# A two-layer decoder trunk on one core: two modulation products are multiplied earlier, with a seventh slot for weights

## The reference

```python
def ada_params(c, w, b):
    return jax.nn.silu(c) @ w + b

def modulate(x, shift, scale):
    return x * (1.0 + scale[:, None, :]) + shift[:, None, :]

def post_norm_residual(x, y, gate, g, b):
    return layer_norm(DEEPNORM_ALPHA * x + (1.0 + gate[:, None, :]) * y, g, b)

def grouped_moe(...):          # 16 experts, 2 per token, both from the best of 4 groups
    ...
    for e in range(N_EXPERTS):
        a = jax.nn.silu(t @ w_gate[e]) * (t @ w_up[e])
        out = out + gates[:, e:e + 1] * (a @ w_down[e])

for l in range(DEPTH):
    mod = ada_params(c, ada_w[l], ada_b[l])
    sh_a, sc_a, g_a, sh_f, sc_f, g_f = jnp.split(mod, 6, axis=-1)
    if l < N_A:
        h = modulate(x, sh_a, sc_a)            # forgetting attention, 16 heads
        ...
    else:
        if l == N_A:
            kv_sh, kv_sc = jnp.split(ada_params(c, kv_ada_w, kv_ada_b), 2, axis=-1)
            hk = modulate(x, kv_sh, kv_sc)     # keys and values of layer 1
            ...
        h = modulate(x, sh_a, sc_a)            # differential attention, 8 heads
        ...
    x = post_norm_residual(x, y, g_a, ln_attn_g[l], ln_attn_b[l])
    h = modulate(x, sh_f, sc_f)
    m = grouped_moe(h, ...)
    x = post_norm_residual(x, m, g_f, ln_ffn_g[l], ln_ffn_b[l])
```

## Time and profile before

| | us |
|---|---|
| median of 3 runs | 898.19 (897.6 to 899.9) |
| the profiled execution | 900.95 |
| its span, of which all rows speak | 899.3 |
| PE busy | 834.7 (93%) |
| DVE busy | 376.0 (42%) |
| transfers, mean rate | 339 GB/s |

### The profile page before, as it was taken

One profiled execution on the slowest core, in us unless ns is written; L12 is line 12 of the kernel. 1 busy time (PEld: TensorE's weight loads), 2 busy tenths in 40 slices (PEclk: granted clock), 3 DMA queues, 4 the chain that ended last, 5 costly groups with the idle time before them and its releaser, 6 DMA issues.

```text
span 899.3 us, 10792 instructions
## 1 busy us (share of the span) xinstructions
PE 834.7 (93%) x3730; PEld 393.0 (44%) x3730; DVE 376.0 (42%) x927; ACT 127.1 (14%) x341; POOL 90.3 (10%) x146
## 2 busy tenths in 40 slices
PE   6899999999998998899979999999999999889984
PEld 3584675435333333333328557654533333333331
DVE  2185867475211221222148688828521122212215
ACT  1001243011100000000010114611110000010010
POOL 1000000051110001011004000215111110000000
PEclk9999999999999999999999999999999999999998
DMA  8999982019999999999999799405499999999901
GB/s 352 431 421 426 399 329 95 1 59 431 426 428 426 425 427 426 427 426 426 425 384 419 299 426 425 175 0 213 163 406 424 428 424 427 426 427 426 392 12 47
DMA packets 23408, 304.59 MB, mean 339 GB/s; under 512 B 2720, under 2 KB 3232, under 8 KB 5280
## 3 DMA queue, kind: packets, MB, share of 16 engines
q1 hardware_dynamic: 22752, 303.14, 80.6%
q10 hardware_dynamic: 576, 0.40, 0.1%
HBM read 302.49 MB, written 1.05 MB: 338 GB/s over the span
## 4 chain that ended last, share of the span: by engine, by line
PE 68%; DMA 21%; DVE 8%; issue 2%; POOL 1%; ACT 1%; POOLq 0%; DVEq 0%; ACTq 0%
PE ps L1724 17%; DMA ring<-in_moe_w_up_dram 12%; PE ps L1732 7%; PE ps L1558 6%; PE ps L1529 6%; PE ps L1542 6%; PE ps L1642 5%; PE ps L1737 4%; DMA stream<-in_moe_w_up_dram 3%; DMA ring<-in_ada_w_dram 3%; DMA ring<-in_moe_w_down_dram 3%; PE ps L1453 1%; PE ps L1431 1%; PE ps L1705 1%; PE ps L1465 1%
## 5 line engine op out<-in xcount | busy, mean ns | idle before, releaser
L1724 PE MATMUL ps<-ring,hT 128*64 128x512 f32 x384 | 172.4, 599 | 11.8 <-DMA ring<-in_moe_w_up_dram 9.9
L1725 PE MATMUL ps<-ring,hT 128*64 128x512 f32 x384 | 172.7, 600 | 0.0
L1233 DVE TENSOR_TENSOR arena<-arena,ps 128x256 f32<-128x256 f32 x32 | 13.5, 421 | 233.8 <-ACT arena L802 126.8
L1724 PEld LDWEIGHTS ps<-ring,hT 128*64 128x64 f32 x384 | 51.1, 138 | 117.4 <-issue 117.4
L1732 PE MATMUL ps<-ring,arena 128*64 128x512 f32 x208 | 94.8, 599 | 0.0
L1733 PE MATMUL ps<-ring,arena 128*64 128x512 f32 x208 | 94.8, 598 | 0.0
L414 DVE SCALAR_TENSOR_TENSOR spare<-ring,csig,spare 128x512 f32<-128x512 f32 x112 | 86.1, 769 | 3.8
L1737 PE MATMUL ps<-arena 128*128 128x512 f32 x144 | 66.6, 605 | 3.2 <-DVE arena L1242 3.2
L1724 PE MATMUL ps<-spare,hT 128*64 128x512 f32 x128 | 58.9, 609 | 2.7 <-DMA stream<-in_moe_w_up_dram 2.5
L1725 PE MATMUL ps<-stream,hT 128*64 128x512 f32 x128 | 58.9, 610 | 0.0
L1529 PE MATMUL ps<-hT,ring 128*128 128x256 f32 x256 | 57.2, 386 | 1.5 <-ACT hT L680 1.5
(11 more groups left out here) (281 smaller groups left out, 1083.3 us busy)
## 6 DMA issues: line engine op xcount, KB each, us to landing
ring<-in_moe_w_down_dram SPq DMA_DIRECT2D x26, 2048.0 KB, 21.8
ring<-in_ada_w_dram SPq DMA_DIRECT2D x24, 2048.0 KB, 14.7
ring<-in_moe_w_gate_dram SPq DMA_DIRECT2D x24, 2048.0 KB, 18.4
ring<-in_moe_w_up_dram SPq DMA_DIRECT2D x24, 2048.0 KB, 21.3
spare<-in_moe_w_gate_dram SPq DMA_DIRECT2D x8, 2048.0 KB, 23.2
stream<-in_moe_w_up_dram SPq DMA_DIRECT2D x8, 2048.0 KB, 25.3
ring<-in_fox_w_in_dram SPq DMA_DIRECT2D x6, 2048.0 KB, 9.8
ring<-in_kv_ada_w_dram SPq DMA_DIRECT2D x4, 2048.0 KB, 13.8
```

Source lines behind the costliest of these rows:

```text
L1724: t.matmul(ps[0:CAP, bank, :], lhs(k), wcols(ng)[:, k, :], start=(k == 0), stop=(k == KC - 1))
L1725: mm = t.matmul(ps[CAP:P, bank, :], lhs(k), wcols(nu)[:, k, :], start=(k == 0), stop=(k == KC - 1))
```

## The change

- Group 4's pieces stand before the first layer's experts in the list, so they are loaded and multiplied (in `turn_stream(0)` and `route(0)`) where group 3 was; group 3 is multiplied among the last heads of the first attention, in two halves.
- The second piece of the output weights, `N_WO[0][1]`, no longer takes a ring slot but a seventh slot (`HALVES`) of four quarters: both rows of `lnw`, the second half of h, and `fold`. It comes in four transfers.
- The rows of norm 0, whose room that is, are loaded in `expert_loads` ahead of piece e3, once that piece is used.
- `gained` takes block 0 first and waits for each block's rows alone; it stands ahead of `number_slots`. `residual` waits in that order.
- ACT modulates all eight chunks of block 0, DVE only the last four of block 1.
- In `turn_stream(1)` four matmuls on constants (`idle_work`) stand in the product's place; `turn_mod(4)` and its `mod_cols` are gone from there.
- The last two pieces of the experts in layer 0 take ring slots, as they did in layer 1, and the rows of norm 1 and the gate bias come ahead of the key weights.
- An overflow round turns `oput` before it folds gate and up, and gates its output with one DVE instruction from a copy, `gate_halves`.

```diff
@@ the list
     ada(3, 0, 1, 2, 3)
     cols(N_WO[0], fox_w_o, 0, 0, 1)
+    ada(4, 0, 1, 2, 3)
     experts_pieces()
-    ada(4, 0, 1, 2, 3)
...
-            if n == first + 3 * NE - (0, SPARES)[l]:
+            if n == first + 3 * NE - SPARES:
                 free = [s for s in free if s < RING]
-        s = free.pop(0)
+        s = HALVES if n == N_WO[0][1] else free.pop(0)
...
+        def quarter_pieces():
+            return [lnw[:, 0, :], lnw[:, 1, :], h[:, 1, :], fold[:, :, :].rearrange("p a n -> p (a n)")]
@@ SP
+            def load_quarters(n):
+                for s_ in range(2):
+                    sp.wait_ge(ht_ready[s_], HT_N[0][s_])
+                sp.wait_ge(f_steps, 1)
+                for q, part_ in enumerate(quarter_pieces()):
+                    sp.dma_start(part_, pieces[n][:, 1024 * q:1024 * q + 1024]).then_inc(full[HALVES], 16)
...
+                        if l == 0 and 6 * i + j == 3:
+                            spent(sp, N_WO[0][1])
+                            norm_rows(0)
...
-                if n == N_WO[0][0]:
-                    norm_rows(0)
...
             gate_bias(2)
+            sp.wait_ge(x_ready, NB)
+            norm_rows(1)
             for n in range(N_MOE[0] + 3 * NE, N_MOE[1]):
-                if n == N_ADA[5][0]:
-                    sp.wait_ge(x_ready, NB)
-                    norm_rows(1)
@@ POOL
-                pool.wait_ge(xn_r, 4 * (norm + 1))
-                for b in (1, 0):
+                for b in range(NB):
+                    pool.wait_ge(xn_r, 4 * norm + 2 * b + 2)
...
             inv_std(0)
+            gained(0)
             number_slots(0)
-            gained(0)
@@ ACT
-                    act.wait_ge(ht_mm, 4 * norm + 2 * b + 1)
-                    for k in range(4):
+                    for k in range(KC if b == 0 else 4):
+                        if k % 4 == 0:
+                            act.wait_ge(ht_mm, 4 * norm + 2 * b + k // 4 + 1)
@@ DVE
                     gate_weights(0, 1, 0)
+                    mod_rows(3)
                     gate_weights(0, 1, 1)
             nothing_added()
             mod_cols(2, 4)
+            mod_cols(3, 7)
             gate_row(1, 5)
-            fold_cols(1)
+            for m in (1, 2):
+                fold_cols(m)
...
-                            for q, rows in enumerate((slice(0, 64), slice(64, P))):
-                                d.tensor_tensor(oy[rows, :], ps[rows, 7, :], gbc[rows, 1, 512 * q:512 * q + 512],
-                                                ALU.mult).then_inc(o_dve, 1)
+                            d.tensor_tensor(oy, ps[:, 7, :], gate_halves, ALU.mult).then_inc(o_dve, 1)
@@ PE
                 if norm == 1:
-                    mod_product(4, range(0, 5))
+                    idle_work(4, 7)
                 for b in range(NB):
                     if b and norm == 0:
-                        mod_product(3, range(0, 2))
-                    if b and norm == 1:
-                        mod_product(4, range(5, KC))
+                        mod_product(4, range(0, 2))
...
-                pe.wait_ge(x_ready, 2 * NB * l + 2 - b)
+                pe.wait_ge(x_ready, 2 * NB * l + b + 1)
...
+                if p == PAIRS_H - 1:
+                    mod_product(3, range(0, 4))
...
             fox_values(PAIRS_H - 3)
+            mod_product(3, range(4, KC))
...
             turn_mod(2, 4)
+            turn_mod(3, 7)
...
             stream_turned(2)
-            turn_mod(4, 0)
```

More of the change, by code:

```diff
@@ L105, in build @@
     SPARES = 2
+    HALVES = RING + SPARES
     SLOT, TURN = [], []
-    turns, free = [0] * (RING + SPARES), list(range(RING))
+    turns, free = [0] * (RING + SPARES + 1), list(range(RING))
     for n in range(len(pieces)):
-        for l, first in enumerate(N_MOE):
+        for first in N_MOE:
             if n == first + RING:
                 free = [RING + i for i in range(SPARES)] + free
-            if n == first + 3 * NE - (0, SPARES)[l]:
+            if n == first + 3 * NE - SPARES:
                 free = [s for s in free if s < RING]
-        s = free.pop(0)
+        s = HALVES if n == N_WO[0][1] else free.pop(0)
         SLOT.append(s)
@@ L238, in build @@
         oy = part(P, 512)
+        gate_halves = part(P, 512)
         oputT = fold[:, 1, 0:S]
@@ L251, in build @@
         ogu = mrow[:, 1, :]
-        full = [sem(f"full{i}") for i in range(RING + SPARES)]
-        used = [sem(f"used{i}") for i in range(RING + SPARES)]
+        full = [sem(f"full{i}") for i in range(RING + SPARES + 1)]
+        used = [sem(f"used{i}") for i in range(RING + SPARES + 1)]
         res_mm = sem("res_mm")
@@ L508, in norm_rows @@
                 if norm % 2:
-                    sp.wait_ge(used[RING], SLOT[:N_MOE[norm // 2] + 3 * NE].count(RING))
+                    sp.wait_ge(used[RING], (norm // 2 + 1) * turns[RING] // DEPTH)
                 for i, w in enumerate(((ln_attn_g, ln_attn_b), (ln_ffn_g, ln_ffn_b))[norm % 2]):
@@ L658, in _ @@
             inv_std(2)
+            gained(2)
             number_slots(1)
-            gained(2)
             windows(1)
@@ L692, in _ @@
                 first_turned(half)
-            def mod_row_out(gi):
-                for n in N_ADA[gi]:
-                    spent(act, n)
-                a.activation(mrow[:, MROW[gi], :], ps[:, mod_bank(gi), :], ACT.Copy).then_inc(mod_row, 1)
             def turned(m):
@@ L826, in _ @@
             router_exp(0)
-            mod_row_out(3)
+            for n in N_ADA[4]:
+                spent(act, n)
+            a.activation(mrow[:, MROW[4], :], ps[:, mod_bank(4), :], ACT.Copy).then_inc(mod_row, 1)
             experts(0)
@@ L955, in turned @@
             def turned(m):
-                norm = M_NORM[m]
-                for b in range(NB):
-                    dve.wait_ge(ht_mm, 4 * norm + 2 * b + 2)
-                    for k in range(4, KC):
-                        modulated(hT[:, k, b * P:(b + 1) * P], turned_bank(b, k), m, k).then_inc(ht_ready[1], 1)
+                dve.wait_ge(ht_mm, 4 * M_NORM[m] + 4)
+                for k in range(4, KC):
+                    modulated(hT[:, k, P:2 * P], turned_bank(1, k), m, k).then_inc(ht_ready[1], 1)
             def turned_again(m):
@@ L1278, in experts @@
                 overflow_tables(l)
+                for q, rows in enumerate((slice(0, 64), slice(64, P))):
+                    link(d.tensor_copy(gate_halves[rows, :], gbc[rows, 1, 512 * q:512 * q + 512]))
                 for i in range(PAIRS):
@@ L1355, in _ @@
             route(0)
-            fold_cols(2)
+            fold_cols(3)
             experts(0)
@@ L1502, in turn_stream @@
                         pe.wait_ge(xn_r, 4 * norm + 2 * b + s_ + 1)
-                        if norm == 1 and b and s_:
-                            pe.wait_ge(mod_row, 4)
                         for k in range(4 * s_, 4 * s_ + 4):
@@ L1659, in route @@
                 if l == 0:
-                    mod_product(3, range(2, 4))
+                    mod_product(4, range(2, 4))
                 else:
@@ L1674, in route @@
                 if l == 0:
-                    mod_product(3, range(4, KC))
+                    mod_product(4, range(4, KC))
                     zeroed((6, 7, 6, 7))
@@ L1769, in overflow @@
                             gate_up_strips(i, j).then_inc(o_pe, 1)
+                            pe.wait_ge(o_dve, k + 3)
+                            for bb in range(NB):
+                                mm = t.transpose(ps[:, 7, bb * P:(bb + 1) * P], oput[:, bb, :], ident[:, :])
+                            mm.then_inc(o_pe, 1)
                             pe.wait_ge(o_act, g * 2 + 1)
-                            pe.wait_ge(o_dve, k + 3)
                             for q in range(4):
@@ L1775, in overflow @@
                             mm.then_inc(o_pe, 1)
-                            for bb in range(NB):
-                                mm = t.transpose(ps[:, 7, bb * P:(bb + 1) * P], oput[:, bb, :], ident[:, :])
-                            mm.then_inc(o_pe, 1)
                             pe.wait_ge(o_dve, k + 6)
```

66 lines of the change are left out of this document (41 added, 25 removed).

## The result

The changed kernel takes 908.68 us (median of 7 runs, 907.6 to 911.8), the kernel before beside it 899.12: a ratio of 1.010, with the 95% interval 1.0075 to 1.0126. It is slower. The prediction, 895.9 with the range 887 to 901.5, is wrong in its sign.

What follows compares the result with a forecast made beforehand. Up to 474 us a transfer queue that starts late and is then full bounds the kernel, afterwards PE. 23.0 - 14.1 - 9.1 - 1.9 = -2.1, with 0.2 for the second routing -2.3: 895.9 us, range 887 to 901.5.

Steps and rivals of the forecast that it cites:

- Attention +4.5: End of first attention: group 3's product among the last heads adds 7.4 and transposes 0.4, 3.2 hidden; 4.5 us longer.
- e2: First expert stage's weight piece, counted from 0, ahead of the norm rows: issued at 202.0, landing at 209.4 us.
- the dear step: First routing: norm rows queued behind e2 land at 212.3, PE waits some 16 us; first expert +23.0 us, attention's 4.5 included.
- First expert stage and behind it: First expert matmul to second layer's key projection: stage -14.1 us as stops go, behind it -9.1 us as group 4 is multiplied.
- Rival (c): First expert stage: refill late, pieces take 5.15 us for 4.95, PE stops 5.2 at e34; +2.9, 901.1 us; chance 0.15.
- e8: First expert stage's weight piece, first after the queue runs dry again: lands 15.4 us after the first expert matmul, before 20.8.
- e34: First expert stage's piece with expert 10's down weights: lands 144.1 us after the first expert matmul, PE there at 144.0.
- gained() in the order 0, 1 frees block 1 last there, but POOL starts one instruction (the iota) sooner and PE asks for it only after its filling matmuls: nothing: Second layer's routing: the new order of the gained rows was claimed to cost nothing.
- Second layer -1.9: Second layer's two overflow rounds: 0.95 us less each, 0.71 for DVE and 0.25 for oput's earlier transposes.

Runs made afterwards that it cites:

- a_early: Changed kernel with the two norm-row loads one place up in SP's order, ahead of transfer e2: 895.31 us against 901.42 for the kernel before, ratio 0.9932.
- a_warm: Changed kernel with idle matmuls in PE's two stops ahead of the second layer's key projection: 905.04 us, ratio 1.0036 to the kernel before.
- a_both: Changed kernel with one wait for both blocks ahead of gained()'s loop, order 0, 1 kept: 901.55 us against 901.42 for the kernel before, ratio 1.0001.
- b_split: Kernel before with only gained()'s order 0, 1, a wait for each block, matching residual waits and number_slots() behind it: 912.22 us against 901.42, ratio 1.0123.
- b_overflow: Kernel before with only the change's overflow rounds (oput transposes first, one operation on gate_halves): 898.02 us against 901.42, ratio 0.997.
- a_both_early: Changed kernel with one wait for both blocks in gained() and the norm rows ahead of e2: 885.67 us, ratio 0.9818 to the kernel before.
- a_halves: Changed kernel with each gained() operation cut into two halves of 512 columns: 905.17 us, ratio 1.006 to the kernel before.
- after_again: Changed kernel unaltered, measured again in a second set of rounds on one chip: 907.51 us against 902.16 for the kernel before, ratio 1.0066.
- a_both_early_halves: Changed kernel with one wait for both blocks, norm rows ahead of e2, and gained() cut into halves: 886.21 us, ratio 0.9864 to the kernel before.

## Why the prediction was wrong

**Attention +4.5: right.** e2 was issued at 201.38 (predicted 202.0), 3.9 us behind its place of before.

**The norm rows, "the dear step" (+23.0): right.** ln_attn_b landed at 211.7 (212.3), POOL worked until 221.2 (222), PE stood 16.27, and the half clock behind it cost 1.5 at the residual (1.9 predicted). A came to 21.65, and in the second set to 20.35. a_early shows the cause: one place in SP's order.

**First expert stage and behind it (-23.2): the mechanism right, the size off by 3.5, in the second set by 2.2.** Rival (c) came in part. The pieces from e8 on took 5.01 us each and not 4.95: e34 landed at 384.04, 1.5 late, and PE stopped 2.35 for it. The half clock behind the stop cost 1.4 more, which no step had: the prediction charged the clock for the stop at the residual and for none later. In the second set (a stop of 1.98 at that place) the clock held, and B is 1.3 shorter. The key projection began 14.2 us behind the stage, 13.7 were predicted. (Before, the prediction placed its start at 474.15, from the chain; the timeline has 473.99.)

**The clock behind the stage: a second term that was missing.** The step compared the times until the key projection starts and took it as unchanged from there. The filling product that was removed had also kept the clock up: C is 2.15 longer, and a_warm gives it back.

**The step that failed: "gained() in the order 0, 1 frees block 1 last there, but POOL starts one instruction (the iota) sooner and PE asks for it only after its filling matmuls: nothing".** It looked at who waits for POOL's result. It did not ask beside what POOL would now run: POOL's first instruction, which before began 1.29 us behind the start of block 1's normalization, begins 0.14 ahead of it. That costs 5.85 us in D, shown by a_both (D back at 31.08 with one wait for both blocks, the order kept) and by b_split (D 36.77 from this part alone). Without it the changed kernel stands at before's time (a_both, 1.0001). The kernel before had the sign of it in the timelines of its first routing, beside the rows that the prediction used:

```profile
195.08 1.25 DVE L1145 TENSOR_TENSOR rt<-rt,st 128x32 f32<-128x32 f32 x1
196.36 0.19 DVE L1146 TENSOR_TENSOR rt<-rt,rb 128x32 f32<-128x32 f32 x1
196.59 2.34 DVE L1118 TENSOR_TENSOR rc<-rt 128x128 f32<-128x128 f32 x1
198.96 0.29 DVE L1119 TENSOR_TENSOR rc<-rt 128x128 f32<-128x128 f32 x1
```

```profile
193.91 2.37 POOL L595 TENSOR_TENSOR stream<-stream,spare 128x1024 f32<-128x1024 f32 x1
```

Equal instructions of 0.19 and 0.29 us take 1.25 and 2.34, and end within 0.15 us of POOL's of 193.91 and 196.36. Why the changed kernel's first routing escaped the same loss can be read too: its rows came so late that POOL started 19 us after the normalization. Its dear step hid a second one, which b_split shows (A +6.1).

**Second layer -1.9: right, but E alone would not show it.** E is 2.24 shorter, a round 1.04. Yet b_split, which has nothing of this part, has E 2.9 shorter. The rows by stretch for E tell the two apart, with the same 1052 records of PE in each (idle is E less PE's busy time; the last column is the time at a granted clock of 0.5):

| kernel | E | PE busy | idle | at half clock |
|---|---|---|---|---|
| before | 245.46 | 233.97 | 11.5 | 6.8 |
| b_split | 242.55 | 230.71 | 11.8 | 0 |
| b_overflow | 241.81 | 232.70 | 9.1 | 3.4 |
| after | 243.22 | 234.08 | 9.1 | 6.8 |
| a_warm | 240.15 | 231.01 | 9.1 | 0 |

With the new overflow rounds the idle time is 8.9 to 9.2 in all ten traces that have them, some 2.4 less than in the two that don't. The busy time goes with the clock alone, up to 3.4 us.

The misses add up: D 6.05, C 2.15, B 3.45, A -1.35 and E -0.34 are 9.96, the way from the forecast -2.3 to the measured +7.66. What stays open is why the pieces took 5.01 us (in the second set too), and why the clock falls in one execution and not in another: the table shows that it makes most of the 3 us by which E differs between nearly equal kernels.

## What to carry to other kernels

When an edit changes when GpSimd works, list what VectorE does in the new stretch and in the old one: the cost is not at GpSimd's own result. In the profile an instruction that takes several times as long as its equals, and ends with an instruction of GpSimd, is the sign; here a wait for both blocks that looked like lost time kept the two apart. When filling work on TensorE goes away, ask what it did for the clock of the stretch behind it, and when a load is moved in a queue, what stands in front of it there. Before a difference of 3 us between two traces is given to an edit, compare their granted clocks.

## What the runs showed of the hardware

- VectorE's instructions that waited for GpSimd's TENSOR_TENSOR: TENSOR_TENSOR with both inputs in SBUF (2.32 instead of 0.29 us), and TENSOR_SCALAR in float32 from SBUF to SBUF (2.48 instead of some 0.5). All 14 normalizations from SBUF, in the twelve traces, that began beside a running instruction of gained() took 1.41 to 2.57 us; the 10 of the same size from PSUM that did took 0.8, as ever. Beside a running GpSimd instruction (196.78 to 199.14 in a_both_early) a TENSOR_REDUCE from PSUM at 198.48 and a TENSOR_TENSOR with one PSUM input at 198.71 took 0.19 each, as ever, and a RECIPROCAL at 199.42, beside the next one, 0.17.
- The waiting instruction comes through between two of GpSimd's: it ended 0.28 us behind the first, and the second was longer by 0.07 (2.41 for 2.34). In a_both_early a TENSOR_TENSOR of VectorE and GpSimd's last instruction both start at 203.98; the first took its usual 0.29, the second 2.50 for 2.35. Cutting GpSimd's work in two cost 1.0 us in 9.5.
- TensorE ran at half clock behind two stops of 1.90 and 1.83 us with 0.66 us of work between them (3.62 us for 1.88), and at full clock behind 0.82 and 0.75 at the same place (a_halves). At e34 the stop's length doesn't tell it: behind 2.35 us (after), 2.00 (a_both_early) and 1.32 (b_overflow) the 16 records took 3.35, 3.51 and 3.40 us, behind 1.98 (after_again) and 1.79 (before) 1.92.
- Equal executions differ by the granted clock: the changed kernel's seven run from 907.59 us at a mean of 0.974 to 911.80 at 0.968, a_both_early_halves' six from 884.46 at 0.991 to 892.48 at 0.979. The 1052 records of E take PE 230.71 us with no time at half clock and 233.97 with 6.8.
